# RWKV mixer of a four-layer backbone on one Trainium2 core: the first half inverse of a layer moved to VectorE, and the two directions' chain steps set half a turn apart

## The reference

```python
def rwkv7_scan(r, w, k, v, kk, a, s0):
    # S_t = S (diag(w) - kk^T (a*kk)) + v^T k ; y_t = S_t r
    def step(s, inp):
        r_t, w_t, k_t, v_t, kk_t, a_t = inp
        s_kk = jnp.einsum('bhvk,bhk->bhv', s, kk_t)
        s = (s * w_t[:, :, None, :] - s_kk[..., None] * (kk_t * a_t)[:, :, None, :]
             + v_t[..., None] * k_t[:, :, None, :])
        return s, jnp.einsum('bhvk,bhk->bhv', s, r_t)
...
for d, f in enumerate((_ident, _flip)):
    yc_d, s_ctx = rwkv7_scan(f(rc), f(wc), f(kc), f(vc), f(kkc), f(ac), s0)
    yl_d, _ = rwkv7_scan(f(rl), f(wl), f(kl), f(vl), f(kkl), f(al), s_ctx)
```

## Time and profile before

| what | us |
|---|---|
| median of three executions | 3631.78 |
| lowest, highest | 3630.01, 3635.14 |
| the profiled execution | 3634.82 |
| its span, first to last instruction | 3633.0 |
| TensorE busy | 3452.8 (95%) |
| VectorE busy | 2489.3 (69%) |
| ScalarE busy | 1155.4 (32%) |
| GpSimd busy | 605.2 (17%) |

### The profile page before, as it was taken

One profiled execution on the slowest core, in us unless ns is written; L12 is line 12 of the kernel. 1 busy time (PEld: TensorE's weight loads), 2 busy tenths in 40 slices (PEclk: granted clock), 3 DMA queues, 4 the chain that ended last, 5 costly groups with the idle time before them and its releaser, 6 DMA issues. The chain is left out here.

```text
span 3633.0 us, 74329 instructions
## 1 busy us (share of the span) xinstructions
PE 3452.8 (95%) x28645; PEld 2516.7 (69%) x28645; DVE 2489.3 (69%) x4512; ACT 1155.4 (32%) x2478; POOL 605.2 (17%) x1193
## 2 busy tenths in 40 slices
PE   7997999999999999999999999999999997888999
PEld 2447778688886455555888866678877546777887
DVE  7975666489897656563898955469987955664431
ACT  3024554233302444431233014323311234663210
POOL 2015554000000323220000000000000115552000
PEclk9998999999999999999999999999999998999999
DMA  6641111143453323223444520044333631111454
GB/s 207 210 136 24 24 24 32 59 136 120 132 161 100 95 86 104 79 79 99 128 125 126 163 81 27 29 124 133 121 122 122 188 109 24 24 24 27 131 153 133
DMA packets 584316, 365.08 MB, mean 100 GB/s; under 512 B 126144, under 2 KB 553480, under 8 KB 581928
## 3 DMA queue, kind: packets, MB, share of 16 engines
q1 hardware_dynamic: 557544, 250.40, 24.9%
q0 software_dynamic: 26432, 110.07, 8.6%
HBM read 348.73 MB, written 11.67 MB: 99 GB/s over the span
## 5 line engine op out<-in xcount | busy, mean ns | idle before, releaser
L274 PE MATMUL PS<-H,WR 128*128 128x512 f32 (+1 forms) x1424 | 477.1, 494 | 0.0
L567 DVE SCALAR_TENSOR_TENSOR WORK<-WORK,SC 128x512 f32<-128x512 f32 x616 | 418.5, 747 | 0.7
L2524 PE MATMUL PS<-WORK 64*64 64x64 f32 (+2 forms) x6944 | 364.3, 233 | 47.9 <-DVE WORK L3127 18.3
L274 PEld LDWEIGHTS PS<-H,WR 128*128 128x128 f32 x1424 | 268.0, 190 | 187.3 <-issue 167.0
L547 POOL DMA_DIRECT2D WORK<-in_ada_w_dram x88 | 66.1, 752 | 1831.1 <-DVE WORK L567 870.8
L2524 PEld LDWEIGHTS PS<-WORK 64*64 64x64 f32 (+1 forms) x6944 | 285.8, 141 | 83.1 <-issue 32.9
L1450 PE MATMUL PS<-BIG,WR 128*128 128x512 f32 (+1 forms) x944 | 329.4, 503 | 5.5 <-DMA WR<-in_rw_wo_dram 2.3
L1450 PEld LDWEIGHTS PS<-BIG,WR 128*128 128x128 f32 x944 | 175.7, 190 | 132.9 <-issue 112.0
L2810 ACT ACTIVATE WORK<-PS 128x64 f32<-128x64 f32 (+3 forms) x528 | 163.4, 326 | 308.1 <-PE PS L2524 303.3
L988 ACT ACTIVATE WORK<-PS 128x512 f32<-128x512 f32 x252 | 134.9, 541 | 340.5 <-PE PS L921 307.2
L921 PE MATMUL PS<-BIG 128*128 128x256 f32 x984 | 223.9, 380 | 0.0
(11 more groups left out here) (359 smaller groups left out, 6403.4 us busy)
## 6 DMA issues: line engine op xcount, KB each, us to landing
WORK<-in_ada_w_dram POOLq DMA_DIRECT2D x88, 1024.0 KB, 6.5
WR<-in_ffn_w_in_dram SPq DMA_DIRECT2D x220, 256.0 KB, 3.0
BIG<-in_ffn_w_in_dram SPq DMA_DIRECT2D x132, 256.0 KB, 3.4
WR<-in_ffn_w_out_dram SPq DMA_DIRECT2D x106, 256.0 KB, 2.9
WR<-in_ssd_w_in_dram SPq DMA_DIRECT2D x96, 256.0 KB, 2.9
BIG<-scratch_dram POOLq DMA_DIRECT2D x8, 2048.0 KB, 8.0
BIG<-in_ffn_w_out_dram SPq DMA_DIRECT2D x36, 256.0 KB, 3.2
BIG<-in_ada_w_dram SPq DMA_DIRECT2D x4, 2048.0 KB, 18.5
```

Source lines behind the costliest of these rows:

```text
L274: mm = pe.matmul(outs, WR[:, slot, k, 0:m], rhs(k), start=first and k == 0, stop=last and k == nk - 1)
L567: lag(vec.scalar_tensor_tensor(ACC3[:, s_], w, by, ACC3[:, s_], ALU.mult, ALU.add), label)
L2524: return pe.matmul(o, lhs, rhs, start=start, stop=stop)
```

## The change

Four things are changed, all in the RWKV mixer.

- **The chain's order.** The second direction's steps stand half a turn behind the first's: W of direction 0, S of direction 1 for the chunk before, U of direction 0, W of direction 1, S of direction 0, U of direction 1. A slot still holds 24 steps; it now begins with W and U of direction 0 with no step of direction 1 between them, and ends with U and S of direction 1.
- **The first half inverse.** In tile 0 of each layer, half 0 is eliminated by VectorE in a new function `first_inverse` with the same 29 instructions, its products in a piece of another tile (FIRST). GpSimd does half 1 as before, now without half 0 ahead of it. SyncE's `inverse_out(0, 0)` waits for VectorE.
- **Places in the slot lists.** Even slots: `R(i,0,0)` moves from k = 1 to 0, `L01` from 0 to 1. Odd slots: `BV` and `BVv` from 17 to 16, `P2e` from 20 to 18, `P3` from 21 to 22, `kf` from 22 to 23.
- **Staging of the first tile.** `bsum` and `bs` come one unit earlier.

```diff
+        FIRST = XB[:, 0:64]
...
-            chain = [(k, 2 * ((h - 1) // 2) + d, 4 * ((h - 1) % 2) + c) for c in range(4) for k in "WUS" for d in range(2)]
+            link = lambda k, d, c: (k, 2 * ((h - 1) // 2) + d, 4 * ((h - 1) % 2) + c)
+            turns = [("W", 0, 0), ("S", 1, -1), ("U", 0, 0), ("W", 1, 0), ("S", 0, 0), ("U", 1, 0)]
+            chain = [link(k, d, c + c0) for c in range(5) for k, d, c0 in turns if c + c0 in range(4) and (c < 4 or k == "S" and d)]
...
-                early += [(1 if i else 20, "E", i, 0), (1, "R", i, 0, 0), (2, "R", i, 0, 1), (9, "H2", both[0], 0),
+                early += [(1 if i else 20, "E", i, 0), (0, "R", i, 0, 0), (2, "R", i, 0, 1), (9, "H2", both[0], 0),
...
-                    early += [(0, "IB", 0, 0), (0, "IB", 0, 1), (0, "kf", 1), (0, "TS", 1)]
+                    early += [(0, "IB0", 0, 0), (0, "IB", 0, 1), (0, "kf", 1), (0, "TS", 1)]
...
-                        (14, "bs"), (17, "BV"), (17, "BVv"), (19, "sd0"), (19, "sd1"), (13, "VT"))]
+                        (14, "bs"), (16, "BV"), (16, "BVv"), (19, "sd0"), (19, "sd1"), (13, "VT"))]
...
-                    late += [(k, n, i - 1) for k, n in ((4, "P1"), (18, "P2"), (20, "P2e"), (21, "P2v"), (21, "P3"))]
+                    late += [(k, n, i - 1) for k, n in ((4, "P1"), (18, "P2"), (18, "P2e"), (21, "P2v"), (22, "P3"))]
...
-                sp.wait_ge(pool_done, C.at(f"{t}.t{i}.ib{s_}"))
+                sp.wait_ge(pool_done if i or s_ else vec_done, C.at(f"{t}.t{i}.ib{s_}"))
...
+            def first_inverse(i, s_):
+                ps = HALF[s_]
+                vec.wait_ge(blocks_loaded, C.at(f"{t}.t{i}.blocks{s_}"))
+                v(vec.memset(BTN[ps, 0:BLK * BLK:BLK + 1], 1.0))
+                for j_ in range(1, BLK - 1):
+                    shape = [Q, BLK - 1 - j_, j_]
+                    below, product = BIJ[ps, j_ + 1:BLK, 0:j_], FIRST[ps, 0:shape[1] * j_].rearrange("p (i j) -> p i j", j=j_)
+                    v(vec.tensor_tensor(product, BIJ[ps, j_ + 1:BLK, j_:j_ + 1].broadcast_to(shape),
+                                        BIJ[ps, j_:j_ + 1, 0:j_].broadcast_to(shape), ALU.mult))
+                    v(vec.tensor_tensor(below, below, product, ALU.add), f"{t}.t{i}.ib{s_}" if j_ == BLK - 2 else None)
```

More of the change, by code:

```diff
@@ L2390, in slot_steps @@
                     late += [(k, n, i + 1) for k, n in (
-                        (0, "L01"), (2, "sc0"), (3, "L23"), (3, "sub0"), (3, "sc1"), (4, "TL"), (4, "sub1"),
+                        (1, "L01"), (2, "sc0"), (3, "L23"), (3, "sub0"), (3, "sc1"), (4, "TL"), (4, "sub1"),
                         (5, "sum1"), (6, "KS"), (7, "KE"), (8, "pn0"), (9, "pr0"), (9, "pn1"), (11, "rm0"), (12, "ax0"),
```

8 lines of the change are left out of this document (4 added, 4 removed).

## The result

The changed kernel took 3640.18 us (median of 17 executions, 3632.29 to 3645.54), the kernel before 3629.80 (17 executions beside it, 3620.92 to 3635.38). The ratio is 1.0028, with an interval of 1.0021 to 1.0036: 10 us slower, where 12 faster was forecast. The profiled execution of the changed kernel has a span of 3638.4 us, 5.4 more than that of before; the profiled execution of before was itself 5.0 us above its median, that of the changed kernel stood at it, so the traces show only half of the 10 us.

What follows compares the result with a forecast made beforehand. TensorE, 95% busy, was taken as the bound, losing time in short stops behind other engines' queues. Terms -5 - 11 + 3 + 1 = -12 us took 3634.8 to 3622.8, less 3.0 for the median: 3620 us, range 3598 to 3640.

Steps and rivals of the forecast that it cites:

- The half turn in layer 0: Steady slot pairs of layer 0: 5.8 us of stops go, 5.1 come; 0.7 won a pair, 5 us in seven pairs.
- six kinds of places: Layer 0 stops expected from the new order: 0.6 + 0.4 + 1.0 + 1.1 + 1.5 + 0.5 = 5.1 us a pair.
- Layer 3: Half turn in layer 3's slot pairs: 1.67 us stop replaced by a W wait of 0.9; 1.5 us won a pair, about 11.
- The loop of the transfers: Layer 3: Gram matrices leave only behind the other half's inverse transfer, so a pair shortened by y makes the spreading wait y longer.
- The clock: TensorE's granted clock in the steady slots, taken as 1.00; an execution differing there would make the forecast void.
- The first half inverse: Slot 0, elimination on VectorE: 28 x 0.31 = 8.7 us, spreading 1.2 us later; 2.0 lost in layer 0, 1.0 in layer 3.
- The upper bound by the port's lock: Slot 0: VectorE and GpSimd products taking turns end the elimination at 286.3 us, with the spreading 4.1 us late.
- Slot 16: Each layer's slot 16: side-by-side steps cost 0.6 and 0.5, a state wait goes; 0.5 us lost per layer, 1 in both.
- The rest, "nothing": Other moves already counted; `bsum` and `bs` of the first tile move under projections where TensorE doesn't wait: no effect.
- The slower one: Rival, chance 0.12: `L01` starts 1.2 us later in even slots, delaying scans and what follows; 13 us slower, 3645.
- The first rival: Chance 0.12: ScalarE and VectorE reach the U copies in time, so places behind VectorE cost little; 3601 us.
- The second: Rival, chance 0.26: VectorE's stretch or layer 3's transfer loop bounds a pair whatever the chain's order; 3632 us.

Runs made afterwards that it cites:

- inverse_alone: Against the kernel before, only the first half inverse moved to VectorE; 3625.1 us, ratio 0.9981 (0.9972-0.9990).
- the best versions: Three kernels with the new staging and half inverse, even slots' chain in old order, `R` and `L01` unmoved, odd-slot variants; 3613 to 3617 us, 0.45% under the kernel before.

## Where the prediction held and where it failed

**What bounds the kernel.** Right: all stops of the earlier trace rows and the large one of the earlier trace rows went, and others came.

**The half turn in layer 0: the failed step.** I priced the stops at six kinds of places at 5.1 us. There they cost, by the rows above with the hidden part added: slot's start 0.51 (forecast 0.6), odd start 0.28 (0.4), first chunk 1.24 (1.0), second chunk W 1.05 (1.1), end of the odd slot 0.40 + 0.96 (1.5), end of the even slot 0.48 + 0.59 (0.5). That is 5.5, so the prices were good as a sum; one, the end of the even slot, came out at twice its value. The step that failed is the count: I had assumed that stops come only at those places. Five more came: S of direction 1 in the third chunk 0.80, Z behind the spreading in the odd slot 0.66, and three of 0.2 to 0.3 (L23, the last W of direction 0, and W in the odd slot), 2.2 us together. 46.4 - 5.8 + 5.5 + 2.2 = 48.3, as measured. I had named VectorE's queue only where a step was moved past an instruction, and had not walked each of the sixteen copies of a pair against the instruction in front of it.

**Layer 3.** The 1.67 gone and a W waiting in its place is right, though that W cost 1.21 + 0.19 = 1.4 us and not 0.9. The pair of slots 6 and 7 won nothing instead of 1.5, by the same failed step: in slot 6 the places that I had named for an even slot cost 0.65, 0.59, 0.48 and 0.59 us, and the ones that I had not named, S of direction 1 in the third chunk and the last W, 0.53 and 0.68. The loop of the transfers, which I had let take half of the gain, took more in some pairs: with the odd slots shorter, the spreading of even slots 2, 8, 10 and 12 came late. Slots 1 to 14 together lost 6 us; how they divide between these transfers and the clock, which was low in 2, 8, 10 and 14, is open.

The clock, which the prediction named only as a spoiler, is a second open point. The prediction took it as 1.00 in the steady slots, but its own have 0.92 in slot 10 of layer 3, so its pair of 45.0 us there is a pair with a fall; without one it is 43.6. After, the clock fell in slots 2, 8, 10, 14 and 16 of layer 3, where before it had fallen in 3, 10 and 15 (and in slot 1 in both). It makes most of the +3.7 of slot 16 (0.88 for 1.00), but slot 15 was 5.4 us shorter, so for the layer as a whole these two traces don't show that the clock cost the changed kernel more: the mean granted clock of all 17 executions is 0.985, as in those of the kernel before.

**The first half inverse: mis-sized, and of the wrong sign.** Forecast +3, measured -6.9. The 29 instructions took 7.0 us, not 8.7: a dependent one started 0.04 us after the end of the one before, where I had taken 0.1 from two wide instructions of the earlier trace rows, and 28 x 0.06 is the whole difference. What came behind was right (8.8 us for 9.0). The spreading, put 1.2 us later at the least, came 0.6 us sooner counted from the slot's start, at 290.6 us in the times of before; below 291 was the prediction's own sign that the price of a product was wrong. Slot 0 itself went down by 1.2 us in layer 0 and 2.2 in layer 3, where +2 and +1 were put; the 3.6 us that inverse_alone won beyond its slots 0 stay open. That nobody waits for GpSimd's half was not quite right: the second spreading had waited for its transfer (0.24 us in layer 0, 0.73 in layer 3), and no longer does. The upper bound by the port's lock was far off: VectorE's products that met GpSimd's took 0.28 to 0.30 instead of 0.20, GpSimd's up to 1.11. The Trainium skill, page "SBUF — State Buffer", section "SBUF: two separate sides", calls that port an exclusive lock; the trace agrees that GpSimd blocks behind VectorE's wide instructions, and shows that the side with the short ones lost under 1 us in all.

**Slot 16.** +1.2 in layer 0, for 0.5.

**The rest, "nothing".** Wrong by 5.8 us (2.5 to 9): the two instructions of `bsum` and `bs` did have TensorE behind them. The row was in the trace and I had not read the stretch ahead of slot 0. "TensorE doesn't wait there" was stated without a row.

**The rivals.** The slower one had the right sign and its signature (even slots longer by more than a microsecond), but its cause is the smaller part: with L01 back 0.65 us of an even slot of layer 0 went and nothing in layer 3, some 3 of its 17 us. The first rival is out: S at the end of an odd slot waits 0.90 us for its copy. The second has a part: in layer 3 the loop of the transfers took up what odd slots had won, and in layer 0 it stands right behind.

The errors had different signs. By the traces the chain came out 31 us above the forecast, inverse and staging 13 below: -12 + 31 - 13 = +6, the span's +5.4. Of the 31, 15 to 16 stand in slots 1 to 15 of layer 0, 12 in those of layer 3, and 4 in slot 16 of both. The half inverse and the staging hid almost half of the chain's error, so the total looks better than the reckoning was.

## What to carry to other kernels

When an order is turned, list every copy that the bound engine waits for with the instruction in front of it on its own engine, all of them, and not only where a step visibly passes another; then move the long instruction behind the copy (here two such moves gave 13 us). Test an order apart from the moves that repair it, for the sum hides both. And read the stretch ahead of the part that you change: the one edit priced at nothing was 6 of the 16 us that the best versions won.
